# The first output projection: eight rows by seven products, two rows plain

## The reference, cut to what matters

```python
return jnp.concatenate([y_m, y_p], -1).astype(u.dtype) @ w_out     # [1280, 2048] @ [2048, 1024]
...
x = x + gate[:, None] * rmsnorm(yx, g_post[l])
if not last:
    ctx = ctx + gate_c * rmsnorm(yc, g_post[l])
```

## Time and profile before

| | |
|---|---|
| median of 3 runs | 3234.52 us (3231.42 to 3238.70) |
| the profiled execution | 3235.28 us, span 3233.5 us |
| PE / PEld / DVE / ACT busy | 3158.2 / 2586.9 / 1961.4 / 1615.9 us |
| first and last matmul of the projection (L2618) | 1090.1 and 1322.9 us |
| mean granted clock of TensorE | 0.993 |

### The profile page before, as it was taken

The page is one execution under the profiler, slowest core; times in us unless marked ns, Lnnn a source line. Parts: engine busy times, 40 slices in busy tenths (PEclk is TensorE's granted clock), DMA queues, the critical chain, the costliest instruction groups (busy, mean ns, idle before and its releaser), DMA issues. The chain is left out here.

```text
span 3233.5 us, 43262 instructions
## 1 busy us (share of the span) xinstructions
PE 3158.2 (98%) x17220; PEld 2586.9 (80%) x17220; DVE 1961.4 (61%) x3056; ACT 1615.9 (50%) x2637; POOL 111.8 (3%) x244
## 2 busy tenths in 40 slices
PE   7999999999999999999999999998998999999998
PEld 5988889898888887887787787886676888878886
DVE  7554444445444557552589563546849888878765
ACT  5343443534433446313688453524735767665455
POOL 2000000000000000000100000000000000000000
PEclk9999999999999999999999999999999999999999
DMA  6202011120532557312400361010053222235664
GB/s 214 71 3 85 30 56 59 43 72 1 169 122 95 200 205 263 116 33 76 119 2 2 101 174 52 27 57 27 1 184 98 84 79 88 82 130 195 232 231 149
DMA packets 202328, 325.72 MB, mean 101 GB/s; under 512 B 29179, under 2 KB 123232, under 8 KB 202000
## 3 DMA queue, kind: packets, MB, share of 16 engines
q1 hardware_dynamic: 180208, 245.04, 23.5%
q0 software_dynamic: 20848, 77.85, 7.0%
q10 hardware_dynamic: 1072, 0.07, 0.0%
HBM read 275.64 MB, written 47.28 MB: 100 GB/s over the span
## 5 line engine op out<-in xcount | busy, mean ns | idle before, releaser
L408 DVE TENSOR_TENSOR W_rounded<-W,W_rounded 128x2048 fp32r<-128x2048 f32 (+2 forms) x151 | 275.1, 1822 | 322.9 <-ACT W_rounded L399 319.3
L399 ACT ACTIVATE W_rounded<-W 128x2048 fp32r<-128x2048 f32 (+1 forms) x139 | 229.6, 1652 | 275.2 <-DMA W<-in_ab_w_in 60.3
L2618 PE MATMUL G<-W_rounded,r_y_rounded 128*128 128x512 f32 x960 | 226.6, 396 | 1.6 <-DVE W_rounded L408 1.1
L2618 PEld LDWEIGHTS G<-W_rounded,r_y_rounded 128*128 128x128 f32 x960 | 179.7, 188 | 44.8 <-DVE W_rounded L408 2.1
L4401 PE MATMUL G<-down_ring_rounded 128*128 128x512 f32 x924 | 212.2, 390 | 2.5 <-DVE down_ring_rounded L4464 2.5
L1178 PE MATMUL G<-W_rounded,HT_rounded 128*128 128x512 f32 x640 | 213.7, 415 | 0.0
L2243 PE MATMUL G<-HT_rounded,W_rounded 128*128 128x512 f32 (+1 forms) x768 | 207.8, 355 | 0.0
L1222 PE MATMUL G<-HT_rounded,W_rounded 128*128 128x512 f32 (+1 forms) x768 | 206.6, 355 | 1.0 <-PEq L673 1.0
L4401 PEld LDWEIGHTS G<-down_ring_rounded 128*128 128x128 f32 x924 | 172.8, 188 | 40.2 <-DVE down_ring_rounded L4464 4.2
L2966 PE MATMUL G<-W_rounded,HT_rounded 128*128 128x512 f32 x640 | 201.2, 395 | 0.0
L2243 PEld LDWEIGHTS G<-HT_rounded,W_rounded 128*128 128x128 f32 x768 | 136.5, 188 | 24.8 <-issue 3.5
(11 more groups left out here) (569 smaller groups left out, 7479.8 us busy)
## 6 DMA issues: line engine op xcount, KB each, us to landing
W<-in_ab_w_out SPq DMA_DIRECT2D x32, 1024.0 KB, 5.6
up_w_in<-in_w_up SPq DMA_DIRECT2D x44, 512.0 KB, 4.4
W<-in_ab_w_in SPq DMA_DIRECT2D x20, 1024.0 KB, 8.7
W<-in_w_mod SPq DMA_DIRECT2D x8, 2048.0 KB, 8.2
x_rows<-r_xt POOLq DMA_DIRECT2D x32, 512.0 KB, 5.3
down_ring<-act_rows SPq DMA_DIRECT2D x25, 512.0 KB, 4.0
W<-in_c_w_out SPq DMA_DIRECT2D x24, 512.0 KB, 6.6
r_xt<-x_rows POOLq DMA_DIRECT2D x24, 512.0 KB, 4.7
```

What stands on the lines that cost most here:

```text
L399: ins = a.activation(self.half(key, True)[:, at], self.half(key, False, False)[:, at], ACT.Copy)
L408: ins = v.tensor_tensor(self.half(key, False)[:, at], self.half(key, False, False)[:, at], self.half(key, True)[:, at].bitcast(F32), ALU.s ...
L2618: ins = pe.matmul(slot(r)[:, n * 512:(n + 1) * 512], x[y], w[z][:, k, n * 512:(n + 1) * 512], start=(kk == 0 and k == 0 and (y, z) == SPLI ...
```

## The change

`out0_part` no longer calls `rows_part`. It computes row blocks 0 to 7 (1024 x 2048 by 2048 x 1024) with the scheme of `down_part`: products P1, P5, P6, P3, P7, P2, P4, in that order, each in four steps of 24 matmuls, 28 steps. A step holds two high and two low pieces, 16 KB, in a ring of slots: the three slots of `W` and one where `x` rows lie later (steps 0 to 19 take slot s % 4), then also two in `HT` and `HT_lo`. Then the two context blocks run plain, eight items of 24 matmuls. Row blocks 0 to 6 are turned after steps 25, 26, 27 and plain items 0, 4, 6, 7; blocks 7, 8 and 9 between the first pairs of `in1`. The scaling of a row moves from DVE to ACT (`scaled`), with one slot for it; a value to turn also has one slot. The waits of `in1` for the stores of `x` move from its start to its ninth pair.

```diff
+    slot = [s % 4 for s in range(20)] + [0, 4, 5, 1, 0, 4, 5, 2]
+    n_loads = {P1: 2, P5: 3, P6: 2, P3: 1, P7: 3, P2: 2, P4: 1}      # of 512 KB each, per step
+    n_sums = {P1: 0, P5: 2, P6: 2, P3: 1, P7: 2, P2: 1, P4: 0}
...
+            if s == 1:
+                pool.left(sp)
+            if s == 2:
+                sp.wait_ge(*old[1])
+            if s == NQ * P5:
+                pool.done(sp)
+            if p not in (P6, P3):
+                free(sp, s)                       # the step that held the slot has ended
+            if P5 <= p <= P7 and s >= NQ * P5 + 2:
+                sp.wait_ge(s_sum, SUM_BASE + summed(s - 2))
...
+        for s in range(NS):
+            load(s)
+            if s == 3:
+                for q in range(NQ):
+                    sp.dma_start(Tm[:, 2 * q:2 * q + 2, :], W[:, 2 * q:2 * q + 2, 0, 0:512]).then_inc(s_yin, 16)
...
+            if 16 <= s < 20:
+                load_y(s - 16)
+        ended(sp, 24)
+        K.load_item(sp)
+        K.load_item(sp)
+        ended(sp, 27)
+        K.load_item(sp)
+        for kk in range(4, KT):
+            load_y(kk)
+            K.load_item(sp)
...
+    def gpsimd(g):
+        ended(g, 19)
+        B.queue(g, ...)
...
+            for m, r in ...:                      # PE, step s: 8 blocks
+                for y, z in SPLIT_PASSES:
+                    ins = pe.matmul(G[:, bank[r], :], x[y][:, m, r * P:(r + 1) * P], w[z][:, m, :], ...)
...
+            if s >= 25:
+                turn(pe, s - 25)
...
+            if kk == 0:
+                turn(pe, 3)
+            if kk == 4:
+                turn(pe, 4)
+            if kk == 6:
+                turn(pe, 5)
+            if kk == 7:
+                turn(pe, 6)
...
+    def plain_hi(a, kk):                          # y piece 128x512, then the item's weights
+        a.activation(HLr[:, t:t + 2, T:R], HT[:, t:t + 2, T:R], ACT.Copy).then_inc(s_hi, 1)
+        K.split_hi(a, plain[kk])
+    def plain_lo(v, kk):                          # the same two on DVE
+    def copy(a, r):                               # left half of row r, PSUM to Y, 512 columns
+    def scale_of(a, ch, r):                       # Square of the row, rstd
+    def scaled(a, ch, r):                         # Square of x, rstd, wait for turn r - 1, xs = x * rstd
+    def gate(v, r):                               # Y = Y * rstd * gg; wait for x in; x = Y + x
...
+        for s in range(2, 26):                    # ACT
+            high(a, s)
...
+        copy(a, 0); scale_of(a, ch, 0); copy(a, 1); scale_of(a, ch, 1); high(a, 26)
+        copy(a, 2); copy(a, 3); scaled(a, ch, 0); scale_of(a, ch, 2); high(a, 27)
+        scale_of(a, ch, 3); plain_hi(a, 0); scaled(a, ch, 1); plain_hi(a, 1); B.act_hi(a, 0)
+        copy(a, 4); copy(a, 5); scaled(a, ch, 2); copy(a, 6); copy(a, 7)
+        B.act_hi(a, 1); scale_of(a, ch, 4); plain_hi(a, 2); B.act_hi(a, 2); scaled(a, ch, 3)
+        scale_of(a, ch, 5); plain_hi(a, 3); scaled(a, ch, 4); B.act_hi(a, 3)
+        plain_hi(a, 4); scale_of(a, ch, 6); plain_hi(a, 5); scaled(a, ch, 5)
+        B.act_hi(a, 4); scale_of(a, ch, 7); plain_hi(a, 6); plain_hi(a, 7)
+        B.act_hi(a, 5); scaled(a, ch, 6); K.split_hi(a, ("aq", 0, 0)); K.split_hi(a, ("aq", 0, 1))
...
+        for s in range(2, 26):                    # DVE
+            sums(v, s + 1)
+            low(v, s)
...
+        gate(v, 0); gate(v, 1); low(v, 26); gate(v, 2); gate(v, 3); low(v, 27)
+        value(v, 0); plain_lo(v, 0); B.vec_lo(v, 0); value(v, 1); plain_lo(v, 1); B.vec_lo(v, 1)
+        value(v, 2); plain_lo(v, 2); B.vec_lo(v, 2); gate(v, 4); plain_lo(v, 3); value(v, 3)
+        B.vec_lo(v, 3); plain_lo(v, 4); gate(v, 5); plain_lo(v, 5); value(v, 4); plain_lo(v, 6)
+        B.vec_lo(v, 4); gate(v, 6); plain_lo(v, 7); value(v, 5); gate(v, 7)
+        K.split_lo(v, ("aq", 0, 0)); B.vec_lo(v, 5); K.split_lo(v, ("aq", 0, 1))
...
+        if n == 0:                                # seam_pe, after pair n of in1
+            turn(pe, 7)
+            pe.wait_ge(B.x_new, 9)
+        if n == 1:
+            turn(pe, 8)
+            pe.wait_ge(B.x_new, 10)
+        if n == 3:
+            turn(pe, 9)
```

More of the change, by code:

```diff
@@ L1717, in tensor @@
                     ins.then_inc(s_item, 1)
[L1718 to L1721, removed]
+            rows.seam_pe(pe, n)
             for j in (2 * n - 2, 2 * n - 1):
@@ new lines, in out0_part @@
+    unit = 4096
+    NP, NQ = 7, 4
+    NS = NP * NQ
+    P1, P5, P6, P3, P7, P2, P4 = range(NP)
+    plain = [("out0", 0, kk) for kk in range(KT)]
+    first = K.pl.items[plain[0]]
+    w_at = [K.offset["W"] + 4 * unit * ((first + n) % 3) for n in range(3)]
+    old = [K.freed_by[K.by_index[first - 3 + n]] for n in (0, 2)]
+    left_at = SBUF_TOP - 4 * KT * R
+    K.HL = nc.alloc_sbuf_tensor_at("HT_lo_1", [P, KT, R], F32R, offset=left_at)
+    HLx = nc.alloc_sbuf_tensor_at("HT_lo_exact", [P, KT, R], F32, offset=left_at)
@@ new lines, in pair, with ended, free, landed @@
+    def pair(s, n):
+        k = 4 * (s % 2) + 2 * n
+        return HT[:, k:k + 2, 512:1024]
+    def ended(eng, s):
+        p, q = divmod(s, NQ)
+        if q < NQ - 1:
+            eng.wait_ge(s_item, (NQ - 1) * p + q + 1)
+        else:
+            eng.wait_ge(s_row, 4 * p + 4)
+    def free(eng, s):
+        if held[s] is not None:
+            ended(eng, held[s])
+    def landed(eng, s):
+        eng.wait_ge(s_in[slot[s]], IN_BASE[slot[s]] + 16 * sum(n_loads[t // NQ] for t in range(s + 1) if slot[t] == slot[s]))
@@ new lines, in value, with scalar, read, back @@
+    def value(v, r):
+        w = int(r >= XT)
+        B.vec_value(v, r, TR, K.amul[:, 1, w, :], K.modc[:, 1, 0:8, w])
+    def scalar(a):
+        ch = Chain(a, K.a_chain, K.an)
+        def read(dst, p, bank, rows):
+            for r in rows:
+                a.wait_ge(s_row, 4 * p + r + 1)
+                a.activation(dst[:, r, :], G[:, bank[r], :], ACT.Copy).then_inc(s_read, 1)
+        def back(rows):
+            for r in rows:
+                a.wait_ge(s_sum_c, C12 + r + 1)
+                a.wait_ge(s_read, READ_P1 + r + 1)
+                a.activation(G[:, bank_c[r], :], first_sum[:, r, :], ACT.Copy).then_inc(s_read, 1)
+        for s in range(2, 26):
+            high(a, s)
+            if s in (6, 7):
+                read(first_sum, P1, bank_a, (0, 1) if s == 6 else (2, 3))
+            if s in (10, 11):
+                read(fifth, P5, bank_c, (0, 1) if s == 10 else (2, 3))
+            if s in (14, 15):
+                read(u2, P6, bank_a, (0, 1) if s == 14 else (2, 3))
+            if s in (18, 19):
+                back((0, 1) if s == 18 else (2, 3))
+        copy(a, 0)
+        scale_of(a, ch, 0)
+        copy(a, 1)
+        scale_of(a, ch, 1)
+        high(a, 26)
+        copy(a, 2)
+        copy(a, 3)
+        scaled(a, ch, 0)
+        scale_of(a, ch, 2)
+        high(a, 27)
+        scale_of(a, ch, 3)
+        plain_hi(a, 0)
+        scaled(a, ch, 1)
+        plain_hi(a, 1)
+        B.act_hi(a, 0)
+        copy(a, 4)
+        copy(a, 5)
+        scaled(a, ch, 2)
+        copy(a, 6)
+        copy(a, 7)
+        B.act_hi(a, 1)
+        scale_of(a, ch, 4)
+        plain_hi(a, 2)
+        B.act_hi(a, 2)
+        scaled(a, ch, 3)
+        scale_of(a, ch, 5)
+        plain_hi(a, 3)
+        scaled(a, ch, 4)
+        B.act_hi(a, 3)
+        plain_hi(a, 4)
+        scale_of(a, ch, 6)
+        plain_hi(a, 5)
+        scaled(a, ch, 5)
+        B.act_hi(a, 4)
+        scale_of(a, ch, 7)
+        plain_hi(a, 6)
+        plain_hi(a, 7)
+        B.act_hi(a, 5)
+        scaled(a, ch, 6)
+        K.split_hi(a, ("aq", 0, 0))
+        K.split_hi(a, ("aq", 0, 1))
+        K.an = ch.n
@@ new lines, in ready_rows, with left, done, seam_pe @@
+    def ready_rows(pe, n):
+        pe.wait_ge(B.ht_lo, n)
+    def left(eng):
+        eng.wait_ge(s_row, 4 * NP)
+    def done(eng):
+        eng.wait_ge(B.ht_lo, NT)
+        eng.wait_ge(B.stored, 16 * XT)
+    def seam_pe(pe, n):
+        if n == 0:
[6 more added lines that the diff above has]
+            turn(pe, 9)
+    def seam_act(a, ch, n):
+        if n == 0:
+            scale_of(a, ch, 8)
+            scaled(a, ch, 7)
+            B.act_hi(a, 6)
+            scale_of(a, ch, 9)
+            scaled(a, ch, 8)
+            B.act_hi(a, 7)
+        if n == 2:
+            B.act_hi(a, 8)
+            scaled(a, ch, 9)
+        if n == 4:
+            B.act_hi(a, 9)
@@ new lines, in seam_vec @@
+    def seam_vec(v, n):
+        if n == 0:
+            gate(v, 8)
+            value(v, 6)
+            B.vec_lo(v, 6)
+            gate(v, 9)
+        if n == 1:
+            value(v, 7)
+            B.vec_lo(v, 7)
+        if n == 2:
+            value(v, 8)
+        if n == 3:
+            B.vec_lo(v, 8)
+        if n == 4:
+            value(v, 9)
+        if n == 5:
+            B.vec_lo(v, 9)
+    rows = Part(sync, gpsimd, tensor, scalar, vector, turn, (8, 9), ready_rows, done, None, left)
```

327 lines of the change are left out of this document (298 added, 29 removed).

## The result

The changed kernel takes **3244.31 us** (median of 11 runs, 3243.11 to 3248.54) against 3235.93 for the kernel before it on the same chips (11 runs, 3231.42 to 3239.49): a ratio of 1.0026, 95% interval 1.0018 to 1.0034. It is slower by 0.26%, where 3227 was forecast, and lies outside the range. Its profiled execution took 3244.28, span 3242.5 (before 3235.28, span 3233.5).

A forecast was written before the change was run, and what follows sets the result against it. PE was taken to bound the kernel, the stage set by number and pace of matmuls. -22.3 - 3.6 - 1.8 + 3.1 + 12.1 + 5.1 = -7.4 from 3235.3 gave 3227.9, 3227 for the median; range 3214 to 3238.

The forecast's parts named there:

- matmuls and pace: In the stage: 864 matmuls for 960, -22.3 us, and 672 of them at 0.2273 us each, -3.6.
- old stalls: In the old stage: 1.8 us of PE stalls go with their code, -1.8.
- turns: Seven turns in the stage and three in `in1` in place of eight and two, 1.0 us each: 0.
- the ring: Product steps: low parts queue behind next step's sums, 1.5 us over three places; step 3 late by 1.5; sum +3.1.
- the tail: From P2's end to `in1`: PE late at turn 3, plain item 6, `in1`, and turns 2 and 6; +12.1 us, 0 to 16.
- the clock: After the three late places of 3 to 4 us: 1.2 GHz stretches, 1.7 us each, +5.1 (0 to 5.1).
- the pace belongs to the stage: Rival: 0.2326 us for all matmuls of the stage, 3231 us, no measurable change; chance 0.12.
- 1096.5 + 6.8 + 4.6: Step 3: ready at 1107.9 after `y`'s stores, landing and DVE pieces; PE could start at 1106.5, 1.5 us late.
- the ring binds: Rival, steps 3 to 7 and 15 to 19: landing of 10 us makes low parts late, 16 us in all, 3243; chance 0.13.
- x rows: gate(3): its `x` block is there 10.4 us after gate(0), DVE asks at about 11.5; 0, against it up to 3.4.
- The clock stays: Rival: the stands are just under what lowers the clock, 3222 us; chance 0.20.
- The orders leave no other way round: Tail: behind the late places, every later `plain_hi` queues on ACT and every later gate on DVE; part of the +12.1.

The follow-up runs named there:

- own_sums: Changed kernel with VectorE making a step's sums just ahead of the same step's low halves, no longer a step ahead: 3233.75 us.
- seam_waits: own_sums plus tail_order, with the context rows' gate row in its own place and loaded earlier, rotation table's load and VectorE's wait for it moved: 3212.04 us.
- one_stand: seam_waits with TensorE waiting ahead of step 12 for step 14's low halves, which puts in one stand: 3219.47 us.
- tail_order: Changed kernel with ScalarE's and VectorE's calls behind the last ring steps reordered, turns of rows 3, 4, 5 behind plain items 1, 3, 5: 3231.07 us.
- rows_before_three: Changed kernel with SyncE waiting for the `y` stores ahead of step 3's loads, not step 4's, and Tm's four loads ahead of step 3's: 3245.40 us.
- items_first: Changed kernel with ScalarE's last eight and VectorE's last ten calls reordered so that plain items 6, 7 and `aq` come first: 3239.10 us.

## Why the prediction was wrong

By the steps of its sum, profiled execution against profiled execution:

| step | forecast | measured |
|---|---|---|
| matmuls and pace | -25.9 | -25.8 |
| old stalls | -1.8 | -1.8 |
| turns | 0 | 0 (-0.8 in the stage, +0.8 in `in1`) |
| the ring | +3.1 | +9.3 |
| the tail | +12.1 | +16.0 |
| the clock | +5.1 | +10.3 |
| the rest of the span | 0 | +0.9 |

- *Matmuls and pace: right.* 864 matmuls; outside stands and slow clock the distances at L2998 have a mean of 0.2273 (638 of them), at L3019 of 0.2328 (168). The rival that the pace belongs to the stage has fallen. Why it differs between places is as open as before.
- *Turns and old stalls: right in sum, misread in part.* The 1.0 of a turn is the duration of its row; by the starts it adds 0.8. So 3.4 and not 1.8 us were left in the old stage. 1.8 of them are its two stands of half a microsecond and more, the other 1.6 are small gaps, and of such gaps the new stage has 1.8.
- *The ring: the step that failed first.* Its mechanism was right, and so were its places (steps 3, 6, 15, 18). Its size at step 3 was not: "1096.5 + 6.8 + 4.6". 1096.5 is the moment in a kernel whose SyncE issues 3.1 MB from 1080.2 to 1082.4. The change itself puts 5 MB on that queue from 1079.7 to 1085.8, so stores that took 3.8 us take 7.6, step 4's loads leave at 1099.99, and DVE starts on them 8.2 later and not 6.8. That is 3.5 + 1.4 of the 5.4 that step 3 stands longer than I said; the rest is that PE is there at 1105.9, not 1106.5. Steps 6, 15 and 18 stand 2.4 where 1.5 was forecast. The rival "the ring binds" came nearest to the time, 3243, by luck, since its mechanism is wrong: own_sums removes the stands with all its bytes in place, and from step 7 to 14 there was none.
- *The tail: right where the hand-overs are ScalarE's and VectorE's, wrong in x rows.* Measured (and forecast): turn 3 3.7 (3.9), item 6 4.5 (4.1), `in1` 3.1 (3.0), turns 2 and 6 1.9 (1.1). What was costed at nothing is turn 1, 2.8: row 3's load left 5.5 us after gate(0) and DVE asked for it 11.7 after, both as forecast, but it landed after 8.5 us and not 4.3. The bound that the prediction worked out against itself, 1.5 to 3.4 late, held it. The rule of the Trainium skill (DMA: Bandwidth & Descriptors, Queues, rings and completion order), that each DMA engine goes round between queues, gave 0 here, and the measurement decides against that 0: with SyncE's 2 MB issued 1 us earlier the load's first packet moved 3.9 us after its issue, while SyncE's queue alone moved 1.36 MB; without them it moved after 1.2 and the load took 4.5 in all. Only after that did both queues move packets side by side. Whether the engines already had POOL's work in those 3.9 us no run here shows.
- *The clock: half of it missed.* I had three stretches of 3.4 us; there are five of 3.4 or 6.8. Two belong to stands that I did not have (step 3, turn 1). And the cost of one was read from two cases that both had the short stretch, though the trace before has stretches of 6.83 us as well, one of them in the window below. seam_waits has none of it and one_stand puts it back. "The clock stays" has fallen.

```profile
1572.20:1579.00 6.80, 5.29 (x32) 4.42 (x30) 4.63 (x13) 3.56 (x10) 1.67 (x7) 0.50 0.29 86
```

- *"The orders leave no other way round."* Of the orders as written this held, the tail came to 16.0. Of the work it does not: tail_order leaves 1.8 with the same instructions, so the stands were the order's and not the scheme's. Stands and slow clock are 35.6 us in the changed kernel, and seam_waits is 32.3 under it, 24 to 26 under the one before.

The 0.9 us outside the stage and the start of `in1` were not looked into. The durations of the engines' own work were right; what failed is what was taken over from the old trace although the change alters it: the moment at which `y` is stored, the landing of row 3, and the length of a slow stretch.

## What to carry to other kernels

A landing time read from a quiet trace is not a constant: when a change adds megabytes to one queue, work out again every small transfer on the others that something waits for, and reckon that it may not start before the backlog has thinned. In a strictly ordered engine never queue work that is ready behind a wait for a load; ask it of each engine, since a wait that is moved off one queue comes up in another. When an engine at 97% is made to do less, count its new stands first. For TensorE add the slow clock: in these kernels stands of 2.8 to 7.6 us mostly came with 2.9 to 6.2 us of work at half clock, a further 1.4 to 3.1 us each.

## What was not expected of the hardware

- Stands of 2.8 to 6.9 us came with 3.41 or 6.83 us at 1.2 GHz with no order by length that these runs show: 2.8 with 3.41, 3.1 with 6.83, 3.7 with 6.83, 4.5 with 3.41, 6.9 with 6.83; 4.1 in one_stand with 6.83. The stretch often begins before the stand ends.
- Of the 32 stands of 2.8 to 7.6 us in this stage and the start of `in1`, in the changed kernel and the ten experiments, 29 have a slow stretch. Three have none: turn 1 of rows_before_three (2.9) and of items_first (2.8), and item 7 of items_first (3.3). The shorter ones, up to 1.7 us, have none. So the same stand can cost its slow clock in one kernel and not in the next, which limits how finely one profiled execution prices an edit.
- Two 640 KB stores took 3.8, 5.6 and 7.6 us where another queue had issued 3, 4 and 5 MB in the 11 us before; a 512 KB load 4.5 and 8.5 with 0 and 2 MB issued 1 us earlier. The first packet moved 1.1, 1.3 and 4.0 us after the issue of the stores, and 1.2 and 3.9 after that of the load.
